# Attention pairs begin one chunk earlier, beside the fourth values' chunk

## The reference, cut to what matters

```
xn = rmsnorm(h)
q, k, v, xr, gr, ga, gb = split(xn @ w_in)
ya = chunked_band_attention(q, k, v) @ w_attn_out      # 16 heads of 64, with a relative bias
xc = causal_depthwise_conv(xr)
r, i = sigmoid(xc @ w_r + b_r), sigmoid(xc @ w_i + b_i)
h_t = a_t * h_(t-1) + sqrt(1 - a_t^2) * i_t * xc_t       # a = exp(-8 r softplus(-lambda)): a scan over time
yb = (h_t * gelu(gr)) @ w_rnn_out
h = h + (sigmoid(ga) * ya + sigmoid(gb) * yb) @ w_o
h = h + (silu(g) * up) @ w_ffn_out                       # g, up from rmsnorm(h) @ w_ffn_in
```

## Time and profile before

| | us |
|---|---|
| median of 3 runs | 1173.46 |
| lowest, highest | 1173.37, 1175.54 |
| the profiled execution | 1173.36 |
| its span | 1171.6 |
| TensorE busy | 1132.1 |
| VectorE busy | 755.1 |
| ScalarE busy | 564.7 |
| GpSimd busy | 213.4 |

### The profile page before, as it was taken

One profiled execution on the slowest core, in us unless ns is written; L12 is line 12 of the kernel. 1 busy time (PEld: TensorE's weight loads), 2 busy tenths in 40 slices (PEclk: granted clock), 3 DMA queues, 4 the chain that ended last, 5 costly groups with the idle time before them and its releaser, 6 DMA issues.

```text
span 1171.6 us, 21872 instructions
## 1 busy us (share of the span) xinstructions
PE 1132.1 (97%) x8900; PEld 1094.6 (93%) x8900; DVE 755.1 (64%) x922; ACT 564.7 (48%) x727; POOL 213.4 (18%) x222
## 2 busy tenths in 40 slices
PE   6999999999999999998999999999989999999997
PEld 6999889999999999998999898899989999888996
DVE  6647875675666543689886677754467657776333
ACT  6446557445444433565734555543345446554331
POOL 1995003202000000155572020000030002000001
PEclk9999999999999999999999999999999999999999
DMA  9665343654565465344500256655535445655441
GB/s 293 201 217 166 122 145 106 218 172 153 183 211 179 144 215 180 109 143 150 181 31 2 73 180 184 200 177 188 180 104 189 164 142 179 196 181 180 179 143 36
DMA packets 154948, 187.34 MB, mean 160 GB/s; under 512 B 6496, under 2 KB 143872, under 8 KB 154880
## 3 DMA queue, kind: packets, MB, share of 16 engines
q1 hardware_dynamic: 151312, 184.06, 48.2%
q10 hardware_dynamic: 3568, 2.31, 0.7%
HBM read 185.29 MB, written 1.07 MB: 159 GB/s over the span
## 4 chain that ended last, share of the span: by engine, by line
PE 84%; DVE 9%; issue 3%; ACT 2%; SPq 1%; DMA 1%; POOL 0%; POOLq 0%; DVEq 0%; ACTq 0%
PE PS L378 19%; PE PS L379 19%; PE PS L380 19%; PE PS L434 10%; PE PS L436 5%; DVE WL L374 2%; ACT WH L365 1%; DVE XHL L531 1%; PE PS L1874 1%; PE PS L723 1%; PE PS L1860 1%; PE PS L1801 1%; PE PS L673 1%; DMA RAW<-in_w_in 1%; PE PS L1733 1%
## 5 line engine op out<-in xcount | busy, mean ns | idle before, releaser
L374 DVE TENSOR_TENSOR WL<-RAW,WH 128x2048 fp32r<-128x2048 f32 x171 | 405.3, 2371 | 240.2 <-ACT WH L365 240.2
L365 ACT ACTIVATE WH<-RAW 128x2048 fp32r<-128x2048 f32 x171 | 326.5, 1910 | 242.4 <-PE PS L380 200.2
L378 PE MATMUL PS<-XHL,WH 128*128 128x256 f32 x1184 | 342.4, 289 | 15.1 <-DVE WL L327 6.9
L379 PE MATMUL PS<-XHL,WH 128*128 128x256 f32 x1184 | 336.5, 284 | 0.0
L380 PE MATMUL PS<-XHL,WL 128*128 128x256 f32 x1184 | 336.4, 284 | 0.0
L378 PEld LDWEIGHTS PS<-XHL,WH 128*128 128x128 f32 x1184 | 228.7, 193 | 20.6 <-DVE XHL L531 10.8
L379 PEld LDWEIGHTS PS<-XHL,WH 128*128 128x128 f32 x1184 | 229.0, 193 | 0.3
L380 PEld LDWEIGHTS PS<-XHL,WL 128*128 128x128 f32 x1184 | 228.6, 193 | 0.0
L378 PE MATMUL PS<-HH,WH 128*128 (+1 forms) x688 | 195.0, 283 | 4.3 <-DVE SG L1653 2.8
L379 PE MATMUL PS<-HL,WH 128*128 (+1 forms) x688 | 194.7, 283 | 0.0
L380 PE MATMUL PS<-HH,WL 128*128 (+1 forms) x688 | 194.7, 283 | 0.0
(11 more groups left out here) (292 smaller groups left out, 1537.4 us busy)
## 6 DMA issues: line engine op xcount, KB each, us to landing
RAW<-in_mlp_w_up SPq DMA_DIRECT2D x32, 1024.0 KB, 5.5
RAW<-in_mlp_w_down SPq DMA_DIRECT2D x32, 1024.0 KB, 4.9
RAW<-in_w_in SPq DMA_DIRECT2D x26, 1024.0 KB, 5.1
RAW<-in_w_ffn_in_pairs SPq DMA_DIRECT2D x22, 1024.0 KB, 5.1
RAW<-in_dn_w_in SPq DMA_DIRECT2D x16, 1024.0 KB, 5.7
RAW<-in_mb_w_in SPq DMA_DIRECT2D x12, 1024.0 KB, 5.2
RAW<-in_w_ffn_out SPq DMA_DIRECT2D x11, 1024.0 KB, 4.9
RAW<-in_w_attn_out SPq DMA_DIRECT2D x4, 1024.0 KB, 5.1
```

The costliest lines, as they stand in the source:

```text
L365: act.activation(WH[:, k], RAW[:, k], ACT.Copy).then_inc(hi_done, 1)
L374: dve.tensor_tensor(WL[:, k], RAW[:, k], WH[:, k].bitcast(F32), ALU.subtract).then_inc(lo_done, 1)
L378: pe.matmul(out, wh, xh, start=start, stop=False, skip_group_check=True)
L379: pe.matmul(out, wh, xl, start=False, stop=False, skip_group_check=True)
```

## The change: what it does

The eight pairs stand beside v3, gr0 to gr3 and gab0 to gab2. A helper, `beside_attention`, lists these eight steps for the three engines.

- TensorE multiplies v0 to v2, then issues the scores of pair 0, then takes the eight steps; v3 keeps its form with tokens on the partitions. In the step of gr0 it waits for the readout of v3 before the values' product of pair 0. The product of pair 7 goes into the step of gab3.
- VectorE reads v3 out behind the scaling of pair 0. The scans move from the steps of gr0 to gr3 being numbers 0 to 3 to their being numbers 1 to 4: each stays beside the same chunk, behind the low part of a pair.
- ScalarE takes the Gelu in the step of gab3, with no merge gates beside it; the merge gates stay in the steps of gab4 to gab7.
- GpSimd's and SyncE's programs are the same.

```
+        def beside_attention():
+            return [Step(seg[name], j, None) for name, j in
+                    [("v", 3)] + [("gr", j) for j in range(4)] + [("gab", j) for j in range(3)]]
 # ScalarE
-            for st in (Step(seg["v"], j, None) for j in range(4)):
+            for st in (Step(seg["v"], j, None) for j in range(3)):
...
-            for st in (Step(seg["gr"] if j < 4 else seg["gab"], j % 4, None) for j in range(8)):
-                n = st.j if st.seg is seg["gr"] else st.j + 4
+            for n, st in enumerate(beside_attention()):
                 split_hi(act, st)
                 attn_exp(act, n)
                 if n:
                     attn_oh(act, n - 1)
                 attn_pt(act, n)
-            for st in (Step(seg["gab"], j, None) for j in range(4, 8)):
+            for st in (Step(seg["gab"], j, None) for j in range(3, 8)):
                 split_hi(act, st)
-                if st.j == 4:
+                if st.j == 3:
                     attn_oh(act, 7)
                     act.activation(GR[:], GR[:], ACT.Gelu_apprx_tanh).then_inc(s_.gl_done, 1)
-                merge_gate(2 * st.j - 8)
-                merge_gate(2 * st.j - 7)
+                else:
+                    merge_gate(2 * st.j - 8)
+                    merge_gate(2 * st.j - 7)
 # VectorE: the loop over v has three steps too
+            for n, st in enumerate(beside_attention()):
                 attn_shift(dve, ch, n)
                 split_lo(dve, st)
                 attn_scale(dve, ch, n)
-                read_out(st, GR[:, 2 * n:2 * n + 2] if n < 4 else GAB[:, 2 * n - 8:2 * n - 6])
-                if n:
-                    attn_ol(dve, n - 1)
-                if n < 4:
-                    scan(n)
+                if n == 0:
+                    read_v(st)
+                    continue
+                read_out(st, GR[:, 2 * n - 2:2 * n] if n < 5 else GAB[:, 2 * n - 10:2 * n - 8])
+                attn_ol(dve, n - 1)
+                if n < 5:
+                    scan(n - 1)
 # TensorE
-            steps(pe, seg["v"], lambda st: multiply(pe, st, XH, XL, tokens_out=True))
+            for st in (Step(seg["v"], j, None) for j in range(3)):
+                multiply(pe, st, XH, XL, tokens_out=True)
             c = seg["v"].first - 1
             pe.wait_ge(freed[c % SLOTS], c // SLOTS + 1)
             pe.wait_ge(s_.gates_done, 16)
             attn_scores(pe, 0)
+            for n, st in enumerate(beside_attention()):
+                multiply(pe, st, XH, XL, tokens_out=(n == 0))
+                if n == 1:
+                    c = seg["gr"].first - 1
+                    pe.wait_ge(freed[c % SLOTS], c // SLOTS + 1)
                 if n:
                     attn_pv(pe, n - 1)
                 attn_turn(pe, n)
                 if n < 7:
                     attn_scores(pe, n + 1)
-            for st in (Step(seg["gab"], j, None) for j in range(4, 8)):
+            for st in (Step(seg["gab"], j, None) for j in range(3, 8)):
                 multiply(pe, st, XH, XL)
-                if st.j == 4:
+                if st.j == 3:
                     attn_pv(pe, 7)
```

More of the change, by code:

```diff
@@ L1739, in _ @@
             attn_scores(pe, 0)
-            for st in (Step(seg["gr"] if j < 4 else seg["gab"], j % 4, None) for j in range(8)):
-                n = st.j if st.seg is seg["gr"] else st.j + 4
-                multiply(pe, st, XH, XL)
+            for n, st in enumerate(beside_attention()):
[3 more added lines that the diff above has]
+                    pe.wait_ge(freed[c % SLOTS], c // SLOTS + 1)
                 if n:
```

## The result

| | before | after |
|---|---|---|
| median of 20 runs each, us | 1173.90 | 1178.32 |
| lowest, highest, us | 1171.37, 1176.59 | 1175.08, 1180.94 |
| the profiled execution, us (its span) | 1173.36 (1171.6) | 1176.16 (1174.4) |
| mean granted clock of the profiled execution | 0.996 | 0.994 |

The ratio of the runs is 1.0031, 95% interval 1.0021 to 1.0040. That is 3.6 us by the means of the 20 runs (1177.91 against 1174.31); the medians lie 4.4 apart. The forecast was 1174.8, range 1173.0 to 1176.6. The median lies 1.7 us above that range, and the chance of slower by over 0.2% had been put at 0.21.

The account below looks back on a forecast made before the run. TensorE, busy 97% of the span, bounds the kernel; only the entry into attention (104 to 124 us) could move. 1173.36+1.36=1174.72, with the median 0.10 above that execution: 1174.8 us, range 1173.0 to 1176.6.

Parts of the forecast that it names:

- Gelu, merge gates and scans: Steps beside the attention pairs: moving the Gelu away from gates gains 0, scans one step later cost 0.
- the new wait for v3's readout: TensorE before the first pair product: readout near 115.6 is over long before; cost 0, without cover 0.6 us.
- the gap: TensorE's wait before pair 0's transposes (L723): transposes at 115.64, wanted at 112.39, so 3.25 us where 1.89 was.
- the term: Entry into attention: the gap grows from 1.89 to 3.25 us, adding +1.36 us to the time.
- the lock's two bounds: Pair 0's bias pass and maximum beside GpSimd's second product: 0 if free, +1.74 us if held until 111.62; 0 taken.
- rival 1: GpSimd's lock also holds the bias pass at the entry: transposes at 117.38, gap 4.99, time 1176.5 us; chance 0.13.
- The clock behind the gap: After the first transposes: one fall of the clock as before, 0 change taken, bounds -1.55 and +1.55 us.
- Rival 3: Behind the entry gap the clock stays low for twice as long, +1.55 us, time 1176.4 us; chance 0.07.
- the basis: Kernel before as starting time: profiled execution 1173.36 us, median of the runs shown 1173.46, 0.10 above it.

Follow-up runs that it names:

- pool_late_before: Kernel before, with GpSimd's two products of RI and MU held back until VectorE's split for gr2 is done; median 1178.59 us, ratio 1.0038.

## Why the prediction was wrong

**Right: where the change acts.** The entry to attention is the only place; 124 to 260 us stayed full, Gelu, merge gates and scans cost nothing, the new wait for v3's readout none.

**Right: the gap.** Transposes were forecast at 115.64 and came at 115.67; the gap at 3.25, and was 3.22; the term at +1.36, and the block's end moved by 1.40. VectorE came forward by less than TensorE. The gap is the solid part of this: it was 3.22 or 3.23 in all three profiles of the changed kernel. That the absolute times agreed to 0.03 is luck, since the transposes stood at 115.67, 115.64 and 114.72 in them.

**Right: the lock's two bounds.** The bias pass was free, at 0 and not +1.74; rival 1 is out. The Trainium skill ("SBUF — State Buffer", "Who interferes with whom") says so for operations without a second SBUF input and outside the two-port modes. The scaling has one SBUF input yet was held in pool_late_before. A measurement goes with it: 128 more columns cost the scaling 348-284=64 ns and the maximum 408-275=133, so the scaling runs in a mode twice as fast. That this is a two-port mode in the Trainium skill's sense is my reading; no run shows the ports. Lines of VectorE in the changed kernel by shape, 124 to 184 us, with mean ns of one:

```profile
L693 DVE TENSOR_REDUCE NMX<-PR 128x1 f32<-128x256 f32 x12 | 4.9, 408 | 0.0
L714 DVE TENSOR_SCALAR PR<-PR,RSUM 128x256 f32<-128x256 f32 x14 | 4.9, 348 | 0.0
L714 DVE TENSOR_SCALAR PR<-PR,RSUM 128x128 f32<-128x128 f32 x13 | 3.7, 284 | 0.2
...
L693 DVE TENSOR_REDUCE NMX<-PR 128x1 f32<-128x128 f32 x12 | 3.3, 275 | 0.0
```

The prediction could have read this: it named only the splits as exposed to GpSimd's work, and the bias pass as a doubt. It did not matter for the change, where the scaling comes 2.9 us after the products' end, but it upset two experiments.

**Wrong: "The clock behind the gap ... I take 0 change".** This is the step that failed. One execution had shown one fall behind 1.9 us and I took it as what that gap always costs, and one fall behind another gap of 3.2 us as what the new one would. Over many runs the clock behind the gap cost 1.3+-0.4 us in the kernel before and 2.5+-0.7 in the changed one (by filling the gaps). The loss over all runs is 1177.35-1174.47=2.9+-0.4 us: 1.3 by the gap, and about 1.5 by a clock that falls more often behind a longer gap, or for twice as long; which of the two weighs more, the profiles are too few to say. The two costs differ by 1.2+-0.8 only, but the mean clocks tell the kernels apart: 0.9948 to 0.9924 is 5.5+-0.7 us more at the lower level, and filling the gaps takes all of it away. At the 0.48 us of above those 5.5 would be 2.6, more than the 1.5 that remain beside the gap; this account closes to within about 1 us and no better. Rival 3 (twice as long, 1176.4) was the nearest and does occur, but at 0.07 was held too unlikely. The median lies 3.5 us above the forecast: 1.5 of it is this step, 1.0 the basis (next paragraph: 1174.47 over many runs against 1173.46), and 1.0 spread, 1178.32 against the mean 1177.35 of all 44. The first 20 runs were slower than the later 24 (1177.91 against 1176.88), by 1.0+-0.6.

**Wrong: the basis.** The 3 runs shown for before (1173.4 to 1175.5) hid a spread of 1171.3 to 1177.9. A good part of it goes with the clock (correlation -0.70 over 96 runs), which falls at several gaps, there or not: at the 2.0 us wait for DOL, untouched by any edit, in 8 of the 14 profiled executions of all runs here. A range around one profiled execution had to hold these for both kernels.

Open: what decides, execution by execution, whether the clock falls behind a given gap; and whether the new order costs something beside its gap, 0.4+-0.6 us on the two chips where both were timed.

## What to carry to other kernels

Moving a consumer earlier helps only if its producer moves as far: compare how far each engine comes forward, here TensorE by 5.76 us and VectorE by 4.40; the difference is added to the gap. A gap of a busy TensorE cost more than its length here, and the longer one the more; price it from many runs, not from one trace. And before an engine's work is moved out of another's way, list every operation that then comes beside it: GpSimd's 4.7 us held whichever split, scaling or scan they met, and cost TensorE nothing only where none of these was due soon.

## What the runs showed of the hardware that was not expected

- One program, one gap of 3.2 us, three profiled executions: no fall of the clock, a fall of 3.4 us and one of 6.8 us; the work behind it took 7.59, 9.15 and 10.08 us. Three more with a gap of 3.2 or 3.3 us at the same place, in edited kernels, gave the same three: 7.60, 9.14 and 10.19 us.
- The other wait of 3.2 us (L1766 before, L1775 after) was followed by a low clock in all 14 profiled executions, twice for 6.8 us, else for 3.4. The prediction read its price there; at the changed gap the clock did otherwise.
- Spare matmuls that fill a gap of 3.2 us to 0.2, with the data due no sooner, gave 2.5+-0.7 us (1177.35 to 1174.87).
- GpSimd's two products took 7.24 us where they took turns with splits and 4.66 to 4.78 where they did not; a scaling of 1.01 us beside them took 5.31, two scans of 1.26 took 3.47.
